# The product that spreads a norm's scales over the partitions: behind the fourth block of the next dense product instead of the second

## The reference, cut to what matters

```
def head_rms_norm(x, w, n_groups):            # rms_norm is this with one group
    y = x32 * lax.rsqrt(jnp.mean(x32 * x32, axis=-1, keepdims=True) + EPS)
    return (y.reshape(shp) * w.astype(F32)).astype(x.dtype)
...
proj = hn @ w_in                              # hn: the normed rows
...
h = swiglu(rms_norm_2(x, ng[0]), ffn_w_gate[l, 0], ffn_w_up[l, 0], ffn_w_down[l, 0])
```

## Time and profile before

| | |
|---|---|
| runs, us | 3476.53, 3486.66, 3487.84 (median 3486.66) |
| profiled execution, us | 3479.5 |
| its span from first to last instruction, us | 3477.7 |
| TensorE busy (PE) | 2912.1 us, 84% |
| VectorE busy (DVE) | 2455.1 us, 71% |
| ScalarE busy (ACT) | 775.0 us, 22% |
| GpSimd busy (POOL) | 626.6 us, 18% |
| mean of what the DMA engines moved | 247 GB/s |
| mean granted TensorE clock, as a share of full speed | 0.927 |

### The profile page before, as it was taken

How to read it: one execution, slowest core, us unless ns; L and a number is a source line. 1 busy time by engine, 2 the same in 40 slices (tenths; PEclk the granted TensorE clock), 3 DMA queues, 4 the chain that set the end, 5 groups by cost and what they waited for, 6 DMA issues and landing times. The chain is left out here.

```text
span 3477.7 us, 45455 instructions
## 1 busy us (share of the span) xinstructions
PE 2912.1 (84%) x17776; PEld 2292.3 (66%) x17776; DVE 2455.1 (71%) x4591; ACT 775.0 (22%) x1982; POOL 626.6 (18%) x520
## 2 busy tenths in 40 slices
PE   8789978777777889677777769998887999998898
PEld 8678963333333689333333329997777999997898
DVE  7262677777777886877777878775436887867686
ACT  4114122222222342122222221013222101023300
POOL 0000014444445100344444540000000000000000
PEclk9899988889888999888899889999999999999999
DMA  6253559999999734899999996543203565652364
GB/s 205 87 183 102 192 208 421 411 411 415 401 403 421 260 117 166 352 415 410 408 419 391 406 394 179 188 146 122 85 5 124 168 194 167 192 171 91 115 194 152
DMA packets 469127, 859.91 MB, mean 247 GB/s; under 512 B 18736, under 2 KB 398512, under 8 KB 402224
## 3 DMA queue, kind: packets, MB, share of 16 engines
q0 software_dynamic: 73728, 536.90, 37.5%
q1 hardware_dynamic: 394896, 319.85, 29.1%
q10 hardware_dynamic: 288, 0.24, 0.0%
HBM read 848.55 MB, written 8.39 MB: 246 GB/s over the span
## 5 line engine op out<-in xcount | busy, mean ns | idle before, releaser
L2477 PE MATMUL banks<-arena,arena 128*128 128x512 f32 x1744 | 913.5, 682 | 356.4 <-ACT arena L2546 356.4
L2477 PEld LDWEIGHTS banks<-arena,arena 128*128 128x128 f32 x1744 | 371.1, 220 | 880.0 <-ACT arena L2546 441.1
L2435 POOL DMA_INDIRECT arena<-in_peer_uv,arena x512 | 621.6, 1214 | 1380.6 <-DVE arena L2663 684.9
L2701 DVE CUSTOM_DVE_ANT_0 arena<-arena,normed 128x1024 f32<-128x1024 f32 x512 | 625.7, 1222 | 234.4 <-DMA arena<-in_peer_uv,arena 232.0
L410 DVE TENSOR_TENSOR weight_ring_part<-weight_ring,weight_high_parts 128x2048 fp32r<-128x2048 f32 (+2 forms) x244 | 539.9, 2213 | 8.4
L3246 PE MATMUL banks<-normed_columns_part,weight_high_parts 128*128 128x256 f32 x1408 | 392.8, 279 | 1.5 <-DVE weight_ring_part L410 1.1
L3247 PE MATMUL banks<-normed_part,weight_high_parts 128*128 128x256 f32 x1408 | 390.9, 278 | 0.0
L3248 PE MATMUL banks<-normed_columns_part,weight_ring_part 128*128 128x256 f32 x1408 | 390.9, 278 | 0.0
L772 PE MATMUL banks<-weight_high_parts,arena_part 128*128 128x256 f32 x1216 | 341.7, 281 | 36.4 <-PEq L350 23.5
L407 DVE CAST weight_high_parts<-weight_ring 128x2048 fp32r<-128x2048 f32 (+2 forms) x244 | 289.8, 1188 | 104.9 <-PE banks L774 82.3
L773 PE MATMUL banks<-weight_ring_part,arena_part 128*128 128x256 f32 x1216 | 339.3, 279 | 0.0
(11 more groups left out here) (574 smaller groups left out, 4354.9 us busy)
## 6 DMA issues: line engine op xcount, KB each, us to landing
weight_ring<-in_ffn_w_gate SPq DMA_DIRECT2D x88, 512.0 KB, 3.7
weight_ring<-in_ffn_w_up SPq DMA_DIRECT2D x88, 512.0 KB, 4.9
weight_ring<-in_ev_w_in SPq DMA_DIRECT2D x33, 1024.0 KB, 5.4
weight_ring<-in_ffn_w_down SPq DMA_DIRECT2D x32, 1024.0 KB, 5.0
weight_ring<-in_od_w_in SPq DMA_DIRECT2D x23, 1024.0 KB, 5.3
weight_ring<-in_xa_wkv SPq DMA_DIRECT2D x16, 1024.0 KB, 5.6
weight_ring<-in_peer_wq SPq DMA_DIRECT2D x16, 1024.0 KB, 5.2
weight_ring<-in_ev_w_out SPq DMA_DIRECT2D x12, 1024.0 KB, 5.4
```

The lines of the kernel that those rows point to most:

```text
L2435: pool.indirect_dma_start(out=ring[:, slot(i, s), :], out_offset=None, in_=table, in_offset=bass.IndirectOffsetOnAxis(ap=index[:, i % 2, s ...
L2477: mm = pe.matmul(k.ps[:, 2 * b + half, :], diag[:, g % 2, s, :], v, start=n == b * PEER_TOPK, stop=n == last_mixed[b])
L2701: dve.tensor_tensor_reduce(out=ring[:, here, 0:D], in0=ring[:, here, 0:D], in1=k.xn[:, i % NB, :], scale=1.0, scalar=0.0, op0=ALU.mult, op ...
```

## The change

The spreading product moves behind the fourth block (m == 3) in `ffn` and in `columns_out`, and behind the second tile (j == 1) in `rows_out`, where no `tensor_then` hook is given. Nothing is added or taken away, and VectorE's, ScalarE's, GpSimd's and SyncE's lists stay word for word the same.

```diff
@@ columns_out, TensorE
                     elif not (paired and m == 1):
                         product(m, range(kc))
-                    if fresh and m == 1:
+                    if fresh and m == (min(3, len(parts) - 1) if tensor_then is None else 1):
                         self.scale_tensor(pe)
@@ rows_out, TensorE
                             if part + step == kc:
                                 mm.then_inc(self.produced.sem, 1)
-                    if fresh and j == 0:
+                    if fresh and j == (min(1, len(widths) - 1) if tensor_then is None else 0):
                         self.scale_tensor(pe)
@@ ffn, TensorE
                 elif m > 1:
                     product(m, range(KC))
-                if m == 1:
+                if m == 3:
                     k.scale_tensor(pe)
```

## The result

The changed kernel is slower: 3518.85 us, median of 4 runs (3513.81 to 3524.43), against 3482.64 of the kernel before (3476.53 to 3487.84, 4 runs). The ratio is 1.0105, with a 95% interval of 1.0077 to 1.0133. The profiled execution after took 3524.43 us (span 3522.6, mean granted clock 0.918), the one before 3479.5 (3477.7, 0.927): 44.9 us between the traces, 36.2 between the medians. The forecast was 3514.

The account below looks back on a forecast made before the run. Neither TensorE (84% busy) nor VectorE (71%) alone was taken as the bound, but short stretches of TensorE waits. 3479.5 + 15.8 shift + 13.3 clock + 2 scores + 3.1 toward the executions' mean gave 3514 us, range 3495 to 3530.

Parts of the forecast that it names:

- The chain: From spread through scales' copy, VectorE's two reads and third tile's split to block 4: 6.9 us feed-forward, 5.4 or 5.9 elsewhere.
- The pauses that go: Ahead of the ten spreads: all 21.7 us of TensorE's pauses go, covered by blocks 2 and 3.
- The shift: Later chain start at the ten places: +20.9 us at block 4, less 5.1 at short products, +15.8 us.
- The gain of 5.1 us at the three short products: At 2662, 3237 and 3104, with no third tile awaited, the next part starts 1.5, 2.6 and 1.0 us sooner.
- The clock behind block 4: Lower granted clock after new pauses at seven places: 1.9 us each, +13.3 us.
- as at 2910: Low bound of the clock's term: no loss, since the clock stayed at 1.00 behind the 3.25 us pause there.
- The 2 us for the first scores: Clock loss behind new 3.9 us pauses ahead of the scores at 2662 and 3237: 1 us each.
- TensorE has no slack to give this back: Behind block 4, TensorE is busy for all 5.44 us per feed-forward tile, so block 4's delay stays.
- Nothing takes their place: Rival: the 21.7 us of pauses at the ten spreads go without new waits, 3461 us; chance 0.03.
- no change: Rival: block 4's delays are swallowed later, for instance by a part waiting for its weights, 3483 us; chance 0.04.
- only the shift: Rival: the clock stays up behind the new pauses ahead of block 4, 3498 us; chance 0.16.
- The worst clock: Rival: clock loss behind the new pauses is 27 us instead of 15.3, 3525 us; chance 0.16.

Follow-up runs that it names:

- fillers: Changed kernel with 38 (feed-forward 52) unread matmuls behind the late spread at the seven places with more than four blocks: 3512.47 us, ratio 1.0090.
- short products: Kernel before with late spread and third tile's split ahead of VectorE's first read, only at products of four or eight blocks: 3481.02 us, ratio 0.9999.
- the split ahead and the spread late: Changed kernel with the third tile's split ahead of VectorE's first read, one later split left to the next turn: 3487.1 us, ratio 1.0019.
- with it early: Kernel before, spread still behind block 1, with the third tile's split ahead of VectorE's first read and one later split deferred: 3486.87 us, ratio 1.0027.

## Why the prediction was right, and where it wasn't

**The chain: right.** Spread to block 4 was put at 6.9, 5.4 and 5.9 us and measured 6.78, 5.32 and 5.79; spread to first score 4.7, measured 4.47. No pause stands ahead of the ten spreads.

**The pauses that go: wrong.** The step "All 21.7 us of pauses go" failed. 11.9 us of them stay, as waits for the second tile's split. The trace of before had the row; it wasn't read:

```profile
2906.68 2.29 DVE L410 TENSOR_TENSOR weight_ring_part<-weight_ring,weight_high_parts 128x2048 fp32r<-128x2048 f32 x1
2908.89 0.16 DVE L676 TENSOR_SCALAR norm_statistics<-norm_statistics 128x2 f32<-128x2 f32 x1
```

Block 2 uses that second tile, and the split ends at 2908.97, only 1.1 us before the spread started at 2910.06. Two instructions were waiting at the same point of TensorE's list, and only the first showed in the waits.

**The shift: mis-sized.** Up to block 4 (or the part behind) the ten places cost 34.1 us, not 15.8. The 18.3 us between them are the 11.9 of kept pauses, some 5 us of a lower clock in block 2 behind three of them (clock 0.62, 4.45 us a block against 2.8, at 2662, 2715 and 3290), and 1.3 at 2101, where the first 24 matmuls ran at a clock of 0.51 (5.24 us, against 3.67 at 0.77 before). The gain of 5.1 us at the three short products didn't come: together they are 1.8 us longer.

**The clock behind block 4: right in size.** 14.8 us by the windows, 14.0 by block 4's length, against 13.3, though not with its bound of 0 "as at 2910". The fillers showed it by removal. The 2 us for the first scores weren't measured; there the clock fell to 0.66 and 0.80. "TensorE has no slack to give this back" holds but for 2.8 us: TensorE's pause at the end of three feed-forwards became shorter (2.67 to 1.57 us at 2101 and 2910, 2.13 to 1.57 at 3290). The Trainium skill (TensorE: Matmul & The Clock Gate, Loop structure matters more than you think) says that a read of PSUM on VectorE doesn't cool TensorE where the next matmuls follow immediately. In this kernel they don't: at all seven places the next block was held by VectorE's list, and the clock fell.

**The sum: the number fits the medians better than its terms fit the trace.** The ten products are 47.5 us longer up to the scores; the terms for them said 29.1 (15.8 and 13.3). The median rose by 36.2. The profiled execution after is the slowest of its four, the one before lay under its kernel's mean, and by the two paces it has 1 us more behind block 4 (4.2 more at 2101, 3.0 less at 1180). With the shift sized rightly the forecast would have been some 18 us higher, 3532, above the measured range. So 3514 was partly luck; the sign and the chain weren't.

**The rivals.** "Nothing takes their place" fell with block 4's waits, "no change" with the table, and "only the shift" with the windows. The worst clock (3525 us) lies inside what the ratio's interval leaves open (3509 to 3529 us), but its term is refuted: 27 us of clock against 14.8 at the seven places and, by the windows, at most 4.3 at the two scores.

## What to carry to other kernels

When an instruction is moved out of a pause, ask what else waits at that point of the queue: list the ready times of everything that the next instructions need, since the trace shows only the first wait. Where two engines both fill the period, moving an entry inside one list gained nothing here. Taking an entry off the list (0.3 us of 5.44, onto an engine that is busy for 22% of the span) came with a gain of 0.3%, which the traces don't locate.

## What the runs showed that wasn't expected

**Two paces at full clock.** Matmuls of one shape, in one loop, at a granted clock of 1.00 and with no wait between them, ran at either of two paces. The feed-forward at 2101 us, in the kernel before and in the changed one:

```profile
2130.00:2180.00 50.00, 50.00 (x444) 50.00 (x442) 44.11 (x56) 4.00 (x10) 0.00 (x0) 1.00 0.65 190
```

```profile
2140.00:2190.00 50.00, 50.00 (x427) 50.00 (x426) 42.55 (x52) 3.69 (x9) 0.00 (x0) 1.00 0.63 186
```

444 matmuls touch the one stretch of 50 us, 427 the other. From start to start that is 113.3 and 117.8 ns, 2.72 and 2.83 us a block; over 40 blocks it makes 4.3 us. Mostly a product keeps its pace until a pause, and may leave the pause with the other, but the pace also changed behind a single start that came 0.05 us late (fillers, 2746.77) or 0.02 us late (short products, 1182.46). Both paces occur in the kernel before, too. What chooses between them wasn't found, and it makes single traces differ by more than the effects of some edits here. Of the matmuls behind block 4 in the seven products with more than four blocks, 771 ran at the slower pace in the kernel before, 1018 in the changed one, 2866 with the split ahead and the spread late, and 3428 with it early; each costs 4.5 ns. One trace of each kernel neither shows nor excludes that the split ahead brings the slower pace.

**The clock doesn't go by the pause's length alone.** In the kernel before, six pauses of 2.37 to 3.27 us stood ahead of spreads. In the 8 us behind the spreads the clock was 0.79, 0.66, 0.64 and 0.79 at 2662, 2715, 3237 and 3290 us, and 1.00 at 2910 and 3104:

```profile
2715.15:2723.15 8.00, 8.00 (x47) 7.82 (x47) 5.23 (x7) 2.08 (x3) 0.00 (x0) 0.66 0.16 48
3104.41:3112.41 8.00, 7.14 (x62) 6.97 (x61) 4.38 (x4) 3.44 (x13) 0.00 (x0) 1.00 0.39 114
```

The prediction had taken 2910 as the example for pauses of this size. Only 3104, with a shorter pause, did as it did.
